# Moving the first copies, roots and transposes at two entries of the transformer blocks

## The chip, the cores and the metric

The kernel runs on one core of a Trainium2 chip. The metric is the device time of one execution in microseconds (us), as the median over several executions. The engines are TensorE (PE in the profile; PEld is its weight load), VectorE (DVE), ScalarE (ACT), GpSimd (POOL) and SyncE (SP), which issues most DMAs.

## The reference, cut to what matters

Two networks are run one behind the other on 512 rows of 1024 floats, all in float32. The first is a convolution layer and a retention layer with residuals, closed by an RMS normalisation. The second is two transformer blocks (`l` = 0, 1) over these rows and, in block 0, over 256 context rows too; each block has attention with local mixers and then a mixture of experts. The places that matter here are the two entries of a block, where rows are normalised, scaled and shifted, and multiplied by `w_in`:

```
return rms_norm(x, final_norm)                 # end of the first network
...
hx = x * (1 + sc1) + sh1                       # entry of block l
hc = ctx * (1 + mod_c[1]) + mod_c[0]
qx, kx, vx, ... = split(hx @ w_in[l])
kc, vc = split(hc @ w_in[l][:, ATTN_WIDTH:...])     # l = 1: context only feeds keys and values
...
y = hier_moe(tokens, ...)                      # end of block l
ctx = layer_norm(ALPHA * ctx + mod_c[5] * y[...], ln2_g[l], ln2_b[l])
x = layer_norm(ALPHA * x + g2 * y[...], ln2_g[l], ln2_b[l])
```

## The kernel before

Each engine has one program written out by hand; they meet only at semaphores, and each works through its program in order. Rows lie in tiles of 128: tiles 0 to 3 are x, tiles 4 and 5 are the context. Tile t is `xr[:, t, :]`, 128 rows by 1024.

Four entries into a half of a block are numbered `q` (0 and 2 are the entries of blocks 0 and 1 ahead of `w_in`; 1 and 3 those ahead of the mixture of experts). At each one every tile goes through the same steps. TensorE turns it in eight transposes of 128x128 (`mod_transposes(q, i_)`, line 1169) into two PSUM banks, 4 and 5 or 6 and 7 by turns for q = 0 and 2. `mod_copy(q, i_)` then scales, shifts and copies the eight blocks into `b_hxT`: for q = 0 ScalarE copies four (line 821) and VectorE four (line 1724); for q = 2 ScalarE copies all eight of tiles 0 to 4, and for the last tile both copy four. TensorE counts these copies (`hx_Ta`, `hx_Td`) before it uses a tile in a product with a chunk of `w_in` (line 1238). A product for a tile's queries is eight matmuls of 128x512 that add up in one bank; the trace has two records for each, so sixteen. Below, T(i) stands for the transposes of the i-th tile of an entry and P(i) for the i-th query product.

**Entry of block 0 (q = 0)**, called stage A below. The tiles are taken in the order 4, 5, 0, 1, 2, 3, since the context needs no statistics. VectorE adds the last product of the first network to the rows (`residual(1)`, line 1554), ScalarE sums squares (lines 722, 723), `rstd(2)` on VectorE (lines 1455, 1458) and `root(2)` on ScalarE (line 727) give the factor of each row, and VectorE multiplies four tiles (line 1654). There are six query products.

**Entry of block 1 (q = 2)**, stage B. `finish_rows` on VectorE has for each tile `stats_of(i_)`: three operations on 1024 columns that combine the two experts' results fetched by DMA into `c_y` (lines 2119 to 2121), two `bn_stats`, one `bn_aggr`, and one small addition (lines 1666 to 1669). ScalarE takes the root (`row_root`, line 828), and `norm(i_)` on VectorE (lines 1675, 1682) finishes the tile, after which its transposes may begin. There are only four query products here (tiles 0 to 3), but all six tiles are turned. Behind the query products come the products for keys and values (`kv`, six of 256 columns) and the rest of `w_in`. TensorE's own order is given by these lines:

```
for n, (c, kind, w, who) in enumerate(outs):
    while turned_tiles < min(n + 2, T):
        mod_transposes(2 * l, turned_tiles)
        turned_tiles += 1
```

Of the kernel before, what the change touches and what calls it, by code (L numbers as in the profile page):

```python
# [22 lines left out]
KD = D // P  # L23
# [90 lines left out]
def build(nc, a, out):  # L114
    ctx = ExitStack()
    with ctx:
# [4 lines left out]
        def sem(name):  # L121
            if name not in made:
                made[name] = ctx.enter_context(nc.semaphore(name))
            return made[name]
# [590 lines left out]
        def _(act):  # L715
# [94 lines left out]
                act.activation(stats[:, 24:28], stats[:, 16:20], ACT.Sqrt).then_inc(sem("ra_sd"), 1)  # L810

            sum_squares(2, mem(W0 + D, D), lambda t: act.wait_ge(sem("op_x"), past("op_x", 1) + 2 * (t + 1)))
            root(2)

            def mod_copy(q, i_):

                t = mod_order(q)[i_]
                g, b = hx_cols(q, int(t >= TX))
                act.wait_ge(sem("hx_t"), past("hx_t", q) + i_ + 1)
                for k in range(blocks_by_act(q, i_)):  # L820
                    m = act.activation(b_hxT[:, k, t * P:(t + 1) * P], bank(mod_bank(q, i_) + k // 4, P, (k % 4) * P),
                                       ACT.Identity, scale=g[:, k:k + 1], bias=b[:, k:k + 1])
                m.then_inc(sem("hx_Ta"), 1)

            def row_root(q, i_):

# [4 lines left out]
            for l in range(LAYERS):  # L831
# [1 line left out]
                nt = len(tiles)  # L833

                if l == 0:
                    for i_ in range(T):
                        mod_copy(0, i_)

                def queries_copied(i_):
# [123 lines left out]
                    outputs_copied(s, last[s], 1)  # L963

                for i_ in range(nt):
                    if l == 0 and i_ >= 2:
                        mod_copy(2, i_ - 2)
                    row_root(2 * l + 1, i_)
                if l == 0:
                    for i_ in range(nt - 2, nt):  # L970
                        mod_copy(2, i_)


        @block.tensor
        def _(pe):
# [196 lines left out]
            for l in range(LAYERS):  # L1172
# [37 lines left out]

                turned_tiles = 0
                for n, (c, kind, w, who) in enumerate(outs):
                    while turned_tiles < min(n + 2, T):
                        mod_transposes(2 * l, turned_tiles)
                        turned_tiles += 1
                    if n <= T:
                        copied = n + 1 if kind == "q" else T - 1 if n < 6 else T
                        pe.wait_ge(sem("hx_Ta"), past("hx_Ta", 2 * l) + copied)
                        pe.wait_ge(sem("hx_Td"), past("hx_Td", 2 * l) + copied)
                    if n == 0 or outs[n - 1][0] != c:  # L1220
                        g = base + c
                        pe.wait_ge(sem(f"st_w{g % 3}"), streamed(g))
                        wc = slot_cols(g)
                    b, m = out_bank(outs, n), last_in(outs, n)
                    if m is not None:
                        whom = outs[m][3]
                        pe.wait_ge(sem(f"in_{whom}"), past(f"in_{whom}", l) + taken(outs, m, whom))
                    for k in range(KD):
                        if kind in ("q", "g"):
                            o, l_, r_ = bank(b), b_hxT[:, k, w * P:(w + 1) * P], wc[:, k, :]  # L1230
                        elif kind == "kv":
                            o, l_, r_ = bank(b, 256), b_hxT[:, k, w * P:(w + 1) * P], wc[:, k, 0:256]
                        else:
                            f, part = w
                            t0, tn, _ = RANGE[part]
                            col = {"cb": 256, "cc": 0, "cx": 256}[kind] + f * P
                            o, l_, r_ = bank(b, tn), wc[:, k, col:col + P], b_hxT[:, k, t0:t0 + tn]
                        m = pe.matmul(o, l_, r_, start=(k == 0), stop=(k == KD - 1))  # L1238
                    m.then_inc(sem("in_mm"), 1)
                    if kind == "g":  # L1240
                        i_ = tiles.index(w)
                        if i_ == 0:
                            pe.wait_ge(sem("in_dve"), past("in_dve", l) + taken(outs, len(outs), "dve"))
                            pe.wait_ge(sem("ws"), past("ws", l) + 16)
                        turn_queries(i_)
                        turn_keys(i_)
                        if i_ >= 1:
                            mix(i_ - 1)
                        for t in more_keys(l, i_):
                            turn_keys(t, i_)  # L1250
                        if i_ >= 2:
                            turn_mixed(i_ - 2)
# [196 lines left out]
        def _(dve):  # L1449
# [197 lines left out]
                r_gate(h - 1)  # L1647
                r_norm(h)
            r_gate(RH - 1)
            residual(1)  # L1650
            rstd(2)
            dve.wait_ge(sem("op_x"), past("op_x", 1) + 8)
            for t in range(TX):
                dve.tensor_scalar(xr[:, t, :], xr[:, t, :], stats[:, 12 + t:13 + t], None, ALU.mult)\
                    .then_inc(sem("row_norm"), 1)

            def finish_rows(q, tiles, first, mod_q, free=None):

                nt = len(tiles)

                def stats_of(i_):
                    first(i_, tiles[i_])
                    for hf in range(2):
                        link(dve.bn_stats(stats[:, 100 + 12 * i_ + 6 * hf:106 + 12 * i_ + 6 * hf],
                                          xr[:, tiles[i_], hf * CW:(hf + 1) * CW]))
                    link(dve.bn_aggr(stats[:, 172 + 2 * i_:174 + 2 * i_], stats[:, 100 + 12 * i_:112 + 12 * i_]))
                    dve.tensor_scalar(stats[:, 184 + i_:185 + i_], stats[:, 173 + 2 * i_:174 + 2 * i_], LN_EPS, None,
                                      ALU.add).then_inc(sem("row_ve"), 1)  # L1670

                def norm(i_):
                    x_t = xr[:, tiles[i_], :]
                    dve.wait_ge(sem("row_sd"), past_rows(q) + i_ + 1)
                    link(dve.reciprocal(stats[:, 196 + i_:197 + i_], stats[:, 190 + i_:191 + i_]))
                    if mod_q is None:
                        link(dve.scalar_tensor_tensor(out=x_t, in0=x_t, scalar=stats[:, 172 + 2 * i_:173 + 2 * i_],
                                                      in1=b_ln[0], op0=ALU.subtract, op1=ALU.mult))
                        dve.scalar_tensor_tensor(out=x_t, in0=x_t, scalar=stats[:, 196 + i_:197 + i_], in1=b_ln[1],
                                                 op0=ALU.mult, op1=ALU.add).then_inc(sem("fin_x"), 1)  # L1680
                        return
                    dve.tensor_scalar(x_t, x_t, stats[:, 172 + 2 * i_:173 + 2 * i_], stats[:, 196 + i_:197 + i_],
                                      ALU.subtract, ALU.mult).then_inc(sem("row_norm"), 1)

                def rows(i_):
                    t = tiles[i_]
                    if free and t >= TX:
                        free()
                    dve.wait_ge(sem("row_norm"), past_norm(mod_q) + i_ + 1)
                    dve.tensor_tensor(b_hx[:, t, :], xr[:, t, :], b_mod[4 if t >= TX else 1], ALU.mult)\  # L1690
                        .then_inc(sem("hx_scaled"), 1)

                if mod_q == 2:
                    dve.sem_inc(sem("hx_Td"), T - 1)
                dve.wait_ge(sem("row_w"), 32 * (q + 1))
                dve.wait_ge(sem("fin_x"), past_full(q) + (TX if q % 2 == 0 else nt))
                for i_ in range(nt):
                    stats_of(i_)
                    if free:
                        if i_ >= 1:  # L1700
                            mod_copy(mod_q, i_ - 1)
                        norm(i_)
                        if 1 <= i_ < nt - 1:
                            rows(i_ - 1)
                        continue
                    if i_ >= 1:
                        norm(i_ - 1)
                if mod_q is None:
                    norm(nt - 1)
                elif mod_q == 2:  # L1710
                    norm(nt - 1)
                    mod_copy(mod_q, nt - 1)
                else:
                    mod_copy(mod_q, nt - 1)
                    for i_ in range(nt - 2, nt):
                        rows(i_)

            def mod_copy(q, i_):
# [7 lines left out]
                                            g[:, k:k + 1], b[:, k:k + 1], ALU.mult, ALU.add)  # L1726
                ins.then_inc(sem("hx_Td"), 1)

            dve.wait_ge(sem("rows_in"), 80)
            for i_ in range(T):  # L1730
                mod_copy(0, i_)
            for l in range(LAYERS):
                tiles, outs = full(l), in_outputs(l)
# [569 lines left out]
```

## Time and profile before

| what | value |
| --- | --- |
| median of 3 runs | 3088.6 us (3087.21 to 3092.43) |
| the profiled execution | 3091.9 us, its span 3090.1 us |
| mean granted TensorE clock | 0.942 of full speed |
| TensorE busy | 2755.0 us, 89% of the span |
| VectorE, ScalarE, GpSimd busy | 1063.4, 460.4, 317.6 us |
| chain that ended last | TensorE 71%, SyncE's queue 12%, DMA 7%, VectorE 5% |

Times in the rows are microseconds from the start of the span. A row of the timeline has the start, the length, the engine, the line, the operation, what it writes and reads, the number of merged instructions, and in brackets the idle time of the engine ahead of it and what ended it. Merged rows of one line can span short pauses between their instructions.

### The profile page before, as it was taken

Reading aid. Unit: us, or ns where it says so; the run is one execution under the profiler, and the core shown is the slowest. Engines: PE = TensorE matmul, PEld = TensorE weight load, DVE = VectorE, ACT = ScalarE, POOL = GpSimd, SP = SyncE. Lnnn points to the kernel's source line nnn. Section 1 sums busy time; section 2 is a strip of 40 time slices with the busy share of each in tenths; the row PEclk is TensorE's granted clock in tenths of the full one; section 3 lists DMA queues with packets and bytes.
Section 4 is the critical chain, followed back from the end, with each engine's and each line's share of the span. In section 5 each row is a group of like instructions: output and inputs, shape, how many; then the busy total and the mean of one; then the engine's idle time right before and its main releaser. Section 6 shows DMA issues by size and latency. Waiting matters only on the chain.

```text
span 3090.1 us, 33083 instructions
## 1 busy us (share of the span) xinstructions
PE 2755.0 (89%) x11436; PEld 1254.1 (41%) x11436; DVE 1063.4 (34%) x2065; ACT 460.4 (15%) x874; POOL 317.6 (10%) x445
## 2 busy tenths in 40 slices
PE   7999999999998999999699977886999688999773
PEld 3444444444444456564433322233555333333221
DVE  5998960330012042455531111115454521111104
ACT  3111130100111010551101100002151000111000
POOL 0101021000000000001122211110000121222110
PEclk9999999999999999899799998997989699999886
DMA  6665341222120311001699999974201799779993
GB/s 232 206 204 178 108 178 56 99 82 82 60 76 1 120 55 46 10 1 70 242 356 363 387 393 392 392 269 181 99 1 50 276 390 371 259 274 365 394 359 131
DMA packets 272218, 603.12 MB, mean 195 GB/s; under 512 B 18437, under 2 KB 43333, under 8 KB 272001
## 3 DMA queue, kind: packets, MB, share of 16 engines
q1 hardware_dynamic: 256864, 580.70, 51.5%
q0 software_dynamic: 15264, 21.24, 2.0%
q8 instruction: 56, 0.92, 0.1%
q14 instruction: 34, 0.27, 0.0%
HBM read 743.04 MB, written 29.20 MB: 250 GB/s over the span
## 4 chain that ended last, share of the span: by engine, by line
PE 71%; SPq 12%; DMA 7%; DVE 5%; issue 2%; ACT 2%; POOL 0%; POOLq 0%; DVEq 0%; ACTq 0%
PE psum L1404 11%; PE psum L1019 11%; PE psum L1106 11%; SPq L657 10%; PE psum L1238 9%; PE psum L1077 7%; DMA arena<-in_w 6%; PE psum L1342 4%; PE psum L1426 4%; PE psum L1285 2%; PE psum L1274 2%; PE psum L1004 1%; PE psum L1127 1%; PE psum L1297 1%; PE psum L1391 1%
## 5 line engine op out<-in xcount | busy, mean ns | idle before, releaser
L1404 PE MATMUL psum<-arena 128*64 128x512 f32 x2656 | 651.2, 636 | 120.2 <-DMA arena<-in_w 118.5
L1404 PEld LDWEIGHTS psum<-arena 128*64 128x64 f32 x2656 | 197.0, 145 | 454.0 <-issue 448.8
L1019 PE MATMUL psum<-arena 128*128 128x512 f32 x768 | 341.2, 600 | 2.6 <-ACTq L754 2.6
L1106 PE MATMUL psum<-arena 128*128 128x512 f32 x768 | 329.9, 592 | 0.8 <-ACT arena L733 0.8
L1426 PE MATMUL psum<-arena 128*64 128x512 f32 x1328 | 301.8, 598 | 0.2 <-issue 0.2
L1503 DVE SCALAR_TENSOR_TENSOR arena<-arena 128x512 f32<-128x512 f32 x451 | 300.2, 749 | 0.0
L1238 PE MATMUL psum<-arena 128*128 128x512 f32 (+1 forms) x800 | 289.6, 522 | 4.2 <-issue 4.2
L1077 PE MATMUL psum<-arena 128*128 128x512 f32 x512 | 224.6, 602 | 5.2 <-POOL arena L2173 4.4
L1106 PEld LDWEIGHTS psum<-arena 128*128 128x128 f32 x768 | 145.8, 190 | 184.2 <-issue 183.2
L1019 PEld LDWEIGHTS psum<-arena 128*128 128x128 f32 x768 | 143.4, 191 | 177.1 <-issue 174.3
L1238 PEld LDWEIGHTS psum<-arena 128*128 128x128 f32 x800 | 152.3, 192 | 128.8 <-issue 121.1
L2082 DVE COPY arena<-psum 128x256 f32<-128x256 f32 x83 | 35.2, 425 | 418.9 <-PE psum L1415 418.7
L2092 DVE SCALAR_TENSOR_TENSOR arena<-arena,psum 64x512 f32<-64x512 f32 x83 | 61.4, 740 | 330.4 <-ACT arena L957 330.4
L1426 PEld LDWEIGHTS psum<-arena 128*64 128x64 f32 x1328 | 96.3, 138 | 191.2 <-issue 191.1
L957 ACT ACTIVATE arena<-psum 64x512 f32<-64x512 f32 x83 | 49.4, 595 | 806.5 <-PE psum L1404 806.5
L1077 PEld LDWEIGHTS psum<-arena 128*128 128x128 f32 x512 | 98.7, 193 | 130.1 <-issue 128.9
L1342 PE MATMUL psum<-arena 128*128 128x512 f32 x320 | 139.2, 594 | 3.4 <-ACT arena L906 3.4
L2075 DVE COPY arena<-psum 128x512 f32<-128x512 f32 x89 | 61.5, 691 | 208.2 <-PE psum L1391 208.2
L2214 POOL DMA_INDIRECT arena<-moe_in,arena x95 | 101.1, 1064 | 83.0 <-POOL arena L2211 80.4
L2211 POOL COPY arena<-arena 128x1 int32 (+1 forms) x95 | 17.8, 188 | 805.2 <-PE psum L1391 759.3
L1285 PE MATMUL psum<-arena 128*128 128x128 f32 x640 | 87.3, 289 | 9.4 <-issue 4.8
L2230 POOL DMA_INDIRECT moe_out<-arena x83 | 85.0, 1024 | 94.9 <-issue 53.9
(279 smaller groups left out, 2051.6 us busy)
## 6 DMA issues: line engine op xcount, KB each, us to landing
arena<-in_w SPq DMA_DIRECT2D x261, 2048.0 KB
arena<-in_w_ada SPq DMA_DIRECT2D x48, 1024.0 KB, 5.2
arena<-in_conv_w_in SPq DMA_DIRECT2D x24, 1024.0 KB
arena<-in_ret_w_in SPq DMA_DIRECT2D x12, 2048.0 KB, 8.0
arena<-in_w_in SPq DMA_DIRECT2D x8, 2048.0 KB, 9.0
arena<-moe_out SPq DMA_DIRECT2D x10, 1024.0 KB, 9.7
arena<-in_conv_w_out SPq DMA_DIRECT2D x4, 2048.0 KB, 11.9
arena<-in_ret_w_out SPq DMA_DIRECT2D x4, 2048.0 KB, 7.8
```

Of the source, the lines that this page charges most:

```text
L657: sp.dma_start(m_w[s][j], ws[j][:, bass.ds(e * kk[j], kk[j]), :], cond=new)\
L1019: m = pe.matmul(bank(b + c), w[:, k, c * P:(c + 1) * P], c_hT[:, k, :], start=(k == 0), stop=(k == KD - 1))
L1077: m = pe.matmul(bank(2 * t + hf), mem(y + S * k + P * t, P), slot_rows(n)[:, k % 4, hf * CW:(hf + 1) * CW], start=(k == 0), stop=(k == KI ...
L1106: m = pe.matmul(bank(4 * (n % 2) + j), l_, r_, start=(k == 0), stop=(k == KD - 1))
L1238: m = pe.matmul(o, l_, r_, start=(k == 0), stop=(k == KD - 1))
L1285: m = pe.matmul(bank(4 + kv, P, hh * P), b_sb[i % 2][:, 4 * kv + hh, c * P:(c + 1) * P], b_dg[i % 2][:, 4 * kv + hh, :], start=True, stop= ...
L1342: m = pe.matmul(bank(2 * (t % 2) + hf), y[:, t * P:(t + 1) * P], slot_rows(base + 4 + k // 4)[:, k % 4, hf * CW:(hf + 1) * CW], start=(k = ...
L1404: m = pe.matmul(bank(2 * s)[part], m_xsT[s][:, at:at + SB], m_w[s][j][:, k, :], start=(k == 0), stop=(k == KD - 1))
L1426: m = pe.matmul(bank(2 * s + 1)[SB * hf:SB * hf + SB], m_hT[s][:, k, :], m_w[s][2][:, k, hf * CW:(hf + 1) * CW], start=(k == 0), stop=(k = ...
L1503: ins = dve.scalar_tensor_tensor(out=acc, in0=u, scalar=w[:, j:j + 1], in1=acc, op0=ALU.mult, op1=ALU.add)
L2214: pool.indirect_dma_start(out=m_xs[s], in_=halves_in, out_offset=None, in_offset=bass.IndirectOffsetOnAxis(m_gi[s], 0), bounds_check=2 * n ...
L2230: pool.indirect_dma_start(out=halves_out, in_=m_y[s], in_offset=None, out_offset=bass.IndirectOffsetOnAxis(m_si[s], 0), bounds_check=4 * n ...
```

## The change

Three things are moved; nothing is computed that was not computed before, and no operation is added or removed.

1. Stage A: VectorE and ScalarE copy the first turned tile (`mod_copy(0, 0)`, tile 4) ahead of `rstd(2)` and `root(2)`, not behind them.
2. Stage B: VectorE normalises tiles 0, 1 and 2 directly behind their own statistics, and no longer one tile later; tiles 3 to 5 as before. On ScalarE the copy of tile 0 now stands ahead of the root of tile 1, the copy of tile 1 ahead of the root of tile 2, and from tile 3 on the root stands ahead of the copy.
3. Stage B: TensorE's T(n+1) stands in the middle of P(n), behind four of its eight matmuls, and not ahead of P(n). Stage A keeps its order there.

```
--- before.py
+++ after.py
@@ -810,7 +810,6 @@
                 act.activation(stats[:, 24:28], stats[:, 16:20], ACT.Sqrt).then_inc(sem("ra_sd"), 1)
 
             sum_squares(2, mem(W0 + D, D), lambda t: act.wait_ge(sem("op_x"), past("op_x", 1) + 2 * (t + 1)))
-            root(2)
 
             def mod_copy(q, i_):
 
@@ -822,6 +821,9 @@
                                        ACT.Identity, scale=g[:, k:k + 1], bias=b[:, k:k + 1])
                 m.then_inc(sem("hx_Ta"), 1)
 
+            mod_copy(0, 0)
+            root(2)
+
             def row_root(q, i_):
 
                 act.wait_ge(sem("row_ve"), past_rows(q) + i_ + 1)
@@ -833,7 +835,7 @@
                 nt = len(tiles)
 
                 if l == 0:
-                    for i_ in range(T):
+                    for i_ in range(1, T):
                         mod_copy(0, i_)
 
                 def queries_copied(i_):
@@ -963,12 +965,13 @@
                     outputs_copied(s, last[s], 1)
 
                 for i_ in range(nt):
-                    if l == 0 and i_ >= 2:
-                        mod_copy(2, i_ - 2)
+                    if l == 0 and 1 <= i_ < 3:
+                        mod_copy(2, i_ - 1)
                     row_root(2 * l + 1, i_)
+                    if l == 0 and i_ >= 3:
+                        mod_copy(2, i_ - 1)
                 if l == 0:
-                    for i_ in range(nt - 2, nt):
-                        mod_copy(2, i_)
+                    mod_copy(2, nt - 1)
 
 
         @block.tensor
@@ -1210,7 +1213,7 @@
 
                 turned_tiles = 0
                 for n, (c, kind, w, who) in enumerate(outs):
-                    while turned_tiles < min(n + 2, T):
+                    while turned_tiles < min(n + 2 if l == 0 or kind != "q" else n + 1, T):
                         mod_transposes(2 * l, turned_tiles)
                         turned_tiles += 1
                     if n <= T:
@@ -1235,6 +1238,9 @@
                             t0, tn, _ = RANGE[part]
                             col = {"cb": 256, "cc": 0, "cx": 256}[kind] + f * P
                             o, l_, r_ = bank(b, tn), wc[:, k, col:col + P], b_hxT[:, k, t0:t0 + tn]
+                        if k == KD // 2 and l == 1 and kind == "q":
+                            mod_transposes(2 * l, turned_tiles)
+                            turned_tiles += 1
                         m = pe.matmul(o, l_, r_, start=(k == 0), stop=(k == KD - 1))
                     m.then_inc(sem("in_mm"), 1)
                     if kind == "g":
@@ -1647,13 +1653,6 @@
                 r_gate(h - 1)
                 r_norm(h)
             r_gate(RH - 1)
-            residual(1)
-            rstd(2)
-            dve.wait_ge(sem("op_x"), past("op_x", 1) + 8)
-            for t in range(TX):
-                dve.tensor_scalar(xr[:, t, :], xr[:, t, :], stats[:, 12 + t:13 + t], None, ALU.mult)\
-                    .then_inc(sem("row_norm"), 1)
-
             def finish_rows(q, tiles, first, mod_q, free=None):
 
 
@@ -1703,7 +1702,9 @@
                         if 1 <= i_ < nt - 1:
                             rows(i_ - 1)
                         continue
-                    if i_ >= 1:
+                    if mod_q == 2 and i_ < 3:
+                        norm(i_)
+                    elif i_ >= (4 if mod_q == 2 else 1):
                         norm(i_ - 1)
                 if mod_q is None:
                     norm(nt - 1)
@@ -1726,8 +1727,16 @@
                                             g[:, k:k + 1], b[:, k:k + 1], ALU.mult, ALU.add)
                 ins.then_inc(sem("hx_Td"), 1)
 
+            residual(1)
+            mod_copy(0, 0)
+            rstd(2)
+            dve.wait_ge(sem("op_x"), past("op_x", 1) + 8)
+            for t in range(TX):
+                dve.tensor_scalar(xr[:, t, :], xr[:, t, :], stats[:, 12 + t:13 + t], None, ALU.mult)\
+                    .then_inc(sem("row_norm"), 1)
+
             dve.wait_ge(sem("rows_in"), 80)
-            for i_ in range(T):
+            for i_ in range(1, T):
                 mod_copy(0, i_)
             for l in range(LAYERS):
                 tiles, outs = full(l), in_outputs(l)
```

Stage A on ScalarE; L722 and L723 are the sums of squares, L727 is the root, L821 (L820 after the change) the copies of turned tiles, L870 and L872 later copies. Before:

```order
L722 ACTIVATE arena<-arena 128x1024 x4
L723 ACTIVATE arena<-arena 128x1
L727 ACTIVATE arena<-arena 128x4
L821 ACTIVATE arena<-psum,arena 128x128 x24
L870 ACTIVATE arena<-psum 128x512
```

and with the change:

```order
L722 ACTIVATE arena<-arena 128x1024 x4
L723 ACTIVATE arena<-arena 128x1
L820 ACTIVATE arena<-psum,arena 128x128 x4
L727 ACTIVATE arena<-arena 128x4
L820 ACTIVATE arena<-psum,arena 128x128 x20
L872 ACTIVATE arena<-psum 128x512
```

Four of the 24 copies, those of tile 4, have moved ahead of the root. VectorE's program changes in the same way around L1455 and L1458.

Stage B on ScalarE; L828 (L830 after the change) is the root of one tile, preceded by a load of its function table, L821 (L820) the copies. Before:

```order
L828 ACT_TABLE_LOAD
L828 ACTIVATE arena<-arena 128x1 x2
L821 ACTIVATE arena<-psum,arena 128x128 x8
L828 ACTIVATE arena<-arena 128x1
L821 ACTIVATE arena<-psum,arena 128x128 x8
L828 ACTIVATE arena<-arena 128x1
L821 ACTIVATE arena<-psum,arena 128x128 x8
L828 ACTIVATE arena<-arena 128x1
L821 ACTIVATE arena<-psum,arena 128x128 x8
L828 ACTIVATE arena<-arena 128x1
L821 ACTIVATE arena<-psum,arena 128x128 x12
```

and with the change:

```order
L830 ACT_TABLE_LOAD
L830 ACTIVATE arena<-arena 128x1
L820 ACTIVATE arena<-psum,arena 128x128 x8
L830 ACTIVATE arena<-arena 128x1
L820 ACTIVATE arena<-psum,arena 128x128 x8
L830 ACTIVATE arena<-arena 128x1 x2
L820 ACTIVATE arena<-psum,arena 128x128 x8
L830 ACTIVATE arena<-arena 128x1
L820 ACTIVATE arena<-psum,arena 128x128 x8
L830 ACTIVATE arena<-arena 128x1
L820 ACTIVATE arena<-psum,arena 128x128 x12
```

The pair of roots without a copy between them has moved from tiles 0 and 1 to tiles 2 and 3.

Stage B on TensorE; L1169 (L1172) are transposes, L1238 (L1244) the products, of 512 columns for queries and 256 for keys and values. Before:

```order
L1169 MATMUL psum<-arena 128x128 x16
L1238 MATMUL psum<-arena 128x512 x8
L1169 MATMUL psum<-arena 128x128 x8
L1238 MATMUL psum<-arena 128x512 x8
L1169 MATMUL psum<-arena 128x128 x8
L1238 MATMUL psum<-arena 128x512 x8
L1169 MATMUL psum<-arena 128x128 x8
L1238 MATMUL psum<-arena 128x512 x8
L1169 MATMUL psum<-arena 128x128 x8
L1238 MATMUL psum<-arena 128x256 x48
```

and with the change:

```order
L1172 MATMUL psum<-arena 128x128 x8
L1244 MATMUL psum<-arena 128x512 x4
L1172 MATMUL psum<-arena 128x128 x8
L1244 MATMUL psum<-arena 128x512 x8
L1172 MATMUL psum<-arena 128x128 x8
L1244 MATMUL psum<-arena 128x512 x8
L1172 MATMUL psum<-arena 128x128 x8
L1244 MATMUL psum<-arena 128x512 x8
L1172 MATMUL psum<-arena 128x128 x8
L1244 MATMUL psum<-arena 128x512 x4
L1172 MATMUL psum<-arena 128x128 x8
L1244 MATMUL psum<-arena 128x256 x48
```

T(0) now stands alone, each of T(1) to T(4) stands between the halves of P(0) to P(3), and T(5) stands ahead of the key and value products as before.

## Rows read from the trace of the kernel before

**Rows 1.** The page: the span, and the chain that ended last by engine.
```profile
span 3090.1 us, 33083 instructions
...
PE 71%; SPq 12%; DMA 7%; DVE 5%; issue 2%; ACT 2%; POOL 0%; POOLq 0%; DVEq 0%; ACTq 0%
```

**Rows 2.** Timeline of TensorE at the entry of block 0 (stage A).
```profile
1094.34 1.94 PE L1169 MATMUL psum<-arena 128*128 128x128 f32 x16 [0.83 <-issue]
1100.53 9.60 PE L1238 MATMUL psum<-arena 128*128 128x512 f32 x16 [4.25 <-issue]
...
1110.84 7.03 PE L1238 MATMUL psum<-arena 128*128 128x512 f32 x16
```

**Rows 3.** Timelines of VectorE and of ScalarE in stage A.
```profile
1096.41 2.74 DVE L1654 TENSOR_SCALAR arena<-arena 128x1024 f32<-128x1024 f32 x4
1099.06 2.64 DVE L1724 TENSOR_SCALAR arena<-psum,arena 128x128 f32<-128x128 f32 x8
1111.04 1.37 DVE L1724 TENSOR_SCALAR arena<-psum,arena 128x128 f32<-128x128 f32 x4 [9.34 <-PE psum L1169]
...
1095.52 0.20 ACT L723 ACTIVATE arena<-arena 128x1 f32<-128x1 f32 x1
...
1111.04 1.51 ACT L821 ACTIVATE arena<-psum,arena 128x128 f32<-128x128 f32 x4 [12.08 <-PE psum L1169]
```

**Rows 4.** Stretches: length, busy by engine (count), granted TensorE clock, DMA share, GB/s.
```profile
1096.30:1100.50 4.20, 0.00 (x0) 0.00 (x1) 4.17 (x10) 2.66 (x8) 0.00 (x0) 0.79 1.04 400
1100.50:1105.60 5.10, 5.07 (x6) 2.17 (x7) 1.20 (x4) 0.00 (x0) 0.00 (x0) 0.50 0.03 12
...
2071.90:2074.20 2.30, 0.01 (x1) 0.00 (x1) 0.69 (x1) 0.16 (x1) 1.26 (x3) 1.00 0.00 0
...
2075.70:2080.00 4.30, 4.26 (x14) 1.48 (x16) 0.76 (x2) 0.00 (x0) 0.74 (x1) 0.69 0.89 282
```

**Rows 5.** Timeline of TensorE at the entry of block 1 (stage B).
```profile
2113.88 1.97 PE L1169 MATMUL psum<-arena 128*128 128x128 f32 x8 [26.35 <-DVE arena L1682]
...
2122.11 9.04 PE L1238 MATMUL psum<-arena 128*128 128x512 f32 x16
2130.98 1.04 PE L1169 MATMUL psum<-arena 128*128 128x128 f32 x8
2131.86 7.03 PE L1238 MATMUL psum<-arena 128*128 128x512 f32 x16
...
2155.08 1.25 PE L1238 MATMUL psum<-arena 128*128 128x256 f32 x5
```

**Rows 6.** Timeline of VectorE in stage B.
```profile
2101.74 1.22 DVE L2119 TENSOR_TENSOR arena<-arena 128x1024 f32<-128x1024 f32 x1 [25.22 <-DMA arena<-moe_out]
...
2107.29 1.21 DVE L2119 TENSOR_TENSOR arena<-arena 128x1024 f32<-128x1024 f32 x1
...
2113.01 0.81 DVE L1682 TENSOR_SCALAR arena<-arena 128x1024 f32<-128x1024 f32 x1
...
2143.03 0.81 DVE L1682 TENSOR_SCALAR arena<-arena 128x1024 f32<-128x1024 f32 x1
```

**Rows 7.** Timeline of ScalarE in stage B.
```profile
2088.27 1.28 ACT L828 ACT_TABLE_LOAD   x1
2107.41 0.20 ACT L828 ACTIVATE arena<-arena 128x1 f32<-128x1 f32 x1 [17.85 <-DVE arena L1669]
...
2115.89 2.90 ACT L821 ACTIVATE arena<-psum,arena 128x128 f32<-128x128 f32 x8 [2.74 <-PE psum L1169]
...
2142.56 0.23 ACT L828 ACTIVATE arena<-arena 128x1 f32<-128x1 f32 x1
```

**Rows 8.** The first chunk of block 1's `w_in`, and TensorE's wait behind stage B.
```profile
L575 SPq DMA_DIRECT2D arena<-in_w_in x1: 379/379/379, 2089.0 to 2089.0; - x1
...
DMA to landing us min/median/max: 9.9/9.9/9.9
...
2168.91 7.20 PEld L1238 LDWEIGHTS psum<-arena 128*128 128x128 f32 x34 [0.25 <-DVE arena L1760]
```

More of the change, by code:

```diff
@@ L812, in _ @@
             sum_squares(2, mem(W0 + D, D), lambda t: act.wait_ge(sem("op_x"), past("op_x", 1) + 2 * (t + 1)))
-            root(2)
             def mod_copy(q, i_):
@@ L823, in mod_copy @@
                 m.then_inc(sem("hx_Ta"), 1)
+            mod_copy(0, 0)
+            root(2)
             def row_root(q, i_):
@@ L835, in _ @@
                 if l == 0:
-                    for i_ in range(T):
+                    for i_ in range(1, T):
                         mod_copy(0, i_)
@@ L965, in _ @@
                 for i_ in range(nt):
-                    if l == 0 and i_ >= 2:
-                        mod_copy(2, i_ - 2)
+                    if l == 0 and 1 <= i_ < 3:
+                        mod_copy(2, i_ - 1)
                     row_root(2 * l + 1, i_)
+                    if l == 0 and i_ >= 3:
+                        mod_copy(2, i_ - 1)
                 if l == 0:
-                    for i_ in range(nt - 2, nt):
-                        mod_copy(2, i_)
+                    mod_copy(2, nt - 1)
         @block.tensor
@@ L1212, in _ @@
                 for n, (c, kind, w, who) in enumerate(outs):
-                    while turned_tiles < min(n + 2, T):
+                    while turned_tiles < min(n + 2 if l == 0 or kind != "q" else n + 1, T):
                         mod_transposes(2 * l, turned_tiles)
@@ L1237, in _ @@
                             o, l_, r_ = bank(b, tn), wc[:, k, col:col + P], b_hxT[:, k, t0:t0 + tn]
+                        if k == KD // 2 and l == 1 and kind == "q":
+                            mod_transposes(2 * l, turned_tiles)
+                            turned_tiles += 1
                         m = pe.matmul(o, l_, r_, start=(k == 0), stop=(k == KD - 1))
@@ L1649, in _ @@
             r_gate(RH - 1)
[L1650 to L1655, printed above, removed]
             def finish_rows(q, tiles, first, mod_q, free=None):
@@ L1705, in finish_rows @@
                         continue
-                    if i_ >= 1:
+                    if mod_q == 2 and i_ < 3:
+                        norm(i_)
+                    elif i_ >= (4 if mod_q == 2 else 1):
                         norm(i_ - 1)
@@ L1727, in mod_copy @@
                 ins.then_inc(sem("hx_Td"), 1)
+            residual(1)
+            mod_copy(0, 0)
+            rstd(2)
+            dve.wait_ge(sem("op_x"), past("op_x", 1) + 8)
+            for t in range(TX):
+                dve.tensor_scalar(xr[:, t, :], xr[:, t, :], stats[:, 12 + t:13 + t], None, ALU.mult)\
+                    .then_inc(sem("row_norm"), 1)
             dve.wait_ge(sem("rows_in"), 80)
-            for i_ in range(T):
+            for i_ in range(1, T):
                 mod_copy(0, i_)
```

## The prediction

> **What bounds the kernel now.** I read the page first: TensorE carries 71% of the chain that ended last in a span of 3090.1 us [rows 1], so a microsecond that TensorE stands idle or slow in a stage is a microsecond of the end, unless a later wait takes it back. Then the timelines of the two stages, engine by engine, to see what TensorE waits for there, and last the granted clock.
>
> Stage A. T(0) and T(1) are turned in 1.94 us from 1094.34, so until 1096.28; P(0) starts at 1100.53 after 4.25 idle [rows 2]. On VectorE the four normalisations (1096.41, 2.74 long) stand ahead of the copies, and the eight copies of the first two tiles run 2.64 from 1099.06 [rows 3]. Four copies take 1.37 [rows 3], so tile 4's are done at 1100.43, and P(0) starts 0.10 later. That is the last-ending wait. In the idle stretch the granted clock falls (mean 0.79), and it is 0.50, or 1.2 GHz, for the next 5.1 us [rows 4]; P(0) takes 9.60 against 7.03 for P(1) [rows 2], so the fall costs 2.57.
>
> Stage B. VectorE starts when the experts' results arrive at 2101.74 and comes to the second tile at 2107.29, a step of 5.55 per tile without its normalisation [rows 6]. T(0) waits for the normalisation of tile 0, which stands behind the statistics of tile 1 and ends at 2113.01 + 0.81 = 2113.82; T(0) starts at 2113.88 [rows 5, 6]. P(0) starts at 2122.11, behind T(1), and from there TensorE has no pause up to the first key product at 2155.08 [rows 5]. So VectorE sets the start and TensorE itself the rest: tile 5 is normalised by 2143.84 [rows 6], eleven microseconds before the key products. The steady step of a query product with one set of transposes is (2155.08 - 2131.86)/3 = 7.74, of which the transposes take 2131.86 - 2130.98 = 0.88 and the product 6.86 [rows 5]. The first transposes take 1.97 at half rate against 1.04 [rows 5].
>
> **Stage A, part by part.** T(0) alone takes 1.04 [rows 5], so it is done at about 1095.38. VectorE, free after the residual, copies its half in 1.37, to 1096.75. ScalarE's last sum of squares and its small copy end at 1095.52 + 0.20 = 1095.72; its half takes 1.51 [rows 3], to 1097.23. P(0) then starts at about 1097.33 instead of 1100.53: 3.20 earlier. The gap falls from 4.25 to 1.05. What I take: with so short a gap the clock stays full, and the 2.57 come back too. Sum of stage A: 5.8; if the clock falls all the same, 3.2.
>
> What is delayed: the statistics of tiles 0 to 3 wait for tile 4's copies. The root goes from before 1096.2 to about 1097.3, the four normalisations to about 1097.7 to 1100.4, and the second tile's copies on VectorE to 1101.8. TensorE wants the first normalised tile at the end of P(0), 1097.33 + 6.86 = 1104.2, and the second tile's copies one T later: cover of 6 and 3 us. Cost nothing; without that cover it would be the 1.4 of the copies moved ahead.
>
> **Stage B, part by part.** VectorE is free after tile 0's statistics at about the same moment as before, and the root of tile 0 starts at 2107.41 [rows 7]. From the start of a root to the end of the normalisation takes 2143.84 - 2142.56 = 1.28 [rows 6, 7]: tile 0 is done at 2108.69 and T(0) starts at 2108.75. ScalarE's copy began 2.01 behind the start of T(0) and took 2.90 [rows 5, 7], so it ends at 2113.66, and P(0) may start at 2113.75, **8.36 earlier**, since T(1) no longer stands ahead of it. Its weights landed at 2089.0 + 9.9 = 2098.9 [rows 8].
>
> From there I follow the chain that ends last, which is no longer TensorE's own. P(0) starts at half rate. The cost of a start was 2.57 in stage A, and 9.75 - 7.74 + 0.93 = 2.94 in stage B with the slow T(1) counted [rows 5]; I take 2.6, all of it in the first half of P(0). That half takes 3.43 + 2.6 and ends at 2119.8, T(1) at 2120.8 (tile 1 is normalised at about 2115.4, so it does not wait). ScalarE copies tile 1 to 2123.75. Only then comes the root of tile 2, whose statistics were ready at about 2120.9: VectorE idles 2.9. Tile 2 is done at 2125.0, tile 3's statistics at 2130.5, its root at 2130.8, and only then does ScalarE copy tile 2, to 2133.7, though T(2) was done at about 2128.5. This is the new stall: P(1) runs 2124.1 to 2131.85 and P(2) starts at 2133.8, after 1.9 idle. From P(2) on VectorE keeps up (tile 3 normalised at 2137.1 for a T(3) wanted at 2137.2, which is tight; tile 4 at 2143.5 for 2145.1), so the key products start at 2133.8 + 2 x 7.74 + 0.88 = 2150.15 against 2155.08: **4.9 earlier**. Of the 8.36, about 0.9 go back to T(1), which now lies behind the start of P(0), 1.9 to the stall, and the rest to the slow clock, which now meets more of the work.
>
> Behind the stage two things could take it back. TensorE waits 0.25 for VectorE's rotation of the first queries at 2168.9 [rows 8]; VectorE reaches it from T(5) through the last tile's copies, so it moves with T(5). The later chunks of weights are asked for as TensorE frees their place, and move too.
>
> Bounds of stage B: if P(0)'s first half and T(1) run wholly at half rate, T(1) ends 1.8 later and 3.1 are left; if the clock falls in the new pause as well, another start of 2.6 is paid and 0.5 is left. If the clock is high from the start, tile 2's root waits for its statistics alone (2120.9), P(2) starts at 2131.0, and 7.7 are gained.
>
> **A rule weighed.** ScalarE's program alternates a root and copies in stage B. In the rows the table is loaded once, 1.28 us at 2088.27, and later roots follow copies with 0.2 us of their own work and no load between [rows 7]. The Trainium skill, "ScalarE: Activation LUTs", section "What ACT_TABLE_LOAD costs", says that every switch to a function of a different set costs a load of about 1.28 us and a drain of about as much again; with the three switches that my chain holds (copy of tile 0, root of tile 2, copy of tile 2) that would be an estimated 8 us, more than stage B gives. The rows decide: root and copy share what is loaded, and the order shows one load there as before. The sum takes nothing for it.
>
> **Sum.** 5.8 + 4.9 = 10.7. Against the profiled execution that is 3091.9 - 10.7 = 3081.2. That execution stands 3.3 above the median, so for a median I predict 3088.6 - 10.7 = **3077.9 us**, 0.35% faster.
>
> **The rivals.**
> *The clock falls in stage A all the same.* In the pause of 2.3 us at 2071.9 TensorE was idle at full clock, and in the stretch from 2075.7 the clock was 0.69 [rows 4]: a pause does not need to be 4 us long. Against it: stage A's pause is half of that. Then the gain is 3.2 + 4.9 = 8.1: 3080.5.
> *Stage B brings little.* The new pause of 1.9 is close to that one of 2.3. If the clock falls in it, or P(0) is slow throughout, stage B brings 0.5 to 3.1, in all 6.3 to 8.9: 3079.7 to 3082.3.
> *A later wait takes stage B back*, so that it gives nothing at the end: TensorE's wait for the rotation would have to grow by what was gained. Then 5.8 are left: 3082.8, within 0.2%. If stage A's clock is lost too, 3085.4. For it speaks only that 0.25 are waited there already.
> *TensorE stays slow in stage B: slower than before.* With P(0) started early and every half product followed by a chance to wait, its work is thinner, and the clock may stay at 1.2 GHz. Each product then costs 6.86 more and each T about 0.93. It decides against the change once the slow stretch holds 10.7/6.86, about 1.6, more products than in my sum. All four products and five T slow cost 4 x 6.86 + 5 x 0.93 - 2.6 = 29.5 more, less 2 for pauses that the slow products swallow: about 3105. Against it: in both stages the clock rose during P(0) [rows 2, 4, 5], and P(0) to P(1) have no pause.
>
> **How the numbers follow.** Chances: the forecast 0.62, with a range of its own from 3075 to 3081; the clock lost in stage A 0.13; stage B short 0.10; a later wait 0.10; slower 0.05. About 0.2%, 6.2 us, is what can be told from no change. The first three are faster by more, save a little of the third; I put 0.83 on faster, 0.12 on the same, 0.05 on slower. The bounds of the terms give gains of 3.7 to 13.5, so 3075.1 to 3084.9; runs of the kernel before lie from 3087.21 to 3092.43, so I widen below and reach to 3072.5, and above to 3084.5, which leaves out the slow case and the edge of the fourth.
>
> **What would show it.** In the new profile's stage A: VectorE and ScalarE copy four blocks each ahead of the root; TensorE's pause ahead of P(0) is about 1 us, P(0) takes about 7.0, and T(2) does not wait. In stage B: T(0) starts about 7.0 behind the first combine; P(0)'s first half about 5 behind T(0); a pause of about 2 ahead of P(2) that ends with ScalarE's copy, and a pause of about 3 on VectorE ahead of tile 2's reciprocal; the first key product about 48.4 behind the first combine, where it was 53.3. The prediction fails if P(0) in either stage is slow for longer than before, if VectorE or a weight chunk holds TensorE behind the stage, or if another stage changes in length.

## The result and the profile after

The kernel with the change takes 3074.84 us in the median of 6 runs (3071.71 to 3081.5), the kernel before 3092.14 in 6 runs beside it (3087.21 to 3092.64). The ratio is 0.995, with a 95% interval from 0.994 to 0.996: 12 to 19 us faster where 10.7 was forecast. Two later comparisons of the same kernel gave 0.996 [0.9947, 0.9974] and 0.9959 [0.9946, 0.9973], about 12.5 us; their intervals, about 8 to 17 us, hold the 10.7.

The timeline of TensorE at the entry of block 0, with the change, answers to [rows 2]:

```profile
1095.28 1.94 PE L1172 MATMUL psum<-arena 128*128 128x128 f32 x16 [0.83 <-issue]
1098.10 7.13 PE L1244 MATMUL psum<-arena 128*128 128x512 f32 x16 [0.88 <-ACT arena L820]
1105.07 1.04 PE L1172 MATMUL psum<-arena 128*128 128x128 f32 x8
1105.94 7.03 PE L1244 MATMUL psum<-arena 128*128 128x512 f32 x16
```

P(0) starts 2.82 behind T(0) where it was 6.19, after a pause of 0.88 that ends with ScalarE's copy, and takes 7.13 instead of 9.60. The start of P(1) is 10.66 behind T(0) where it was 16.50: **5.84 gained**. The VectorE and ScalarE timelines of the same place answer to [rows 3]:

```profile
1096.39 1.36 DVE L1725 TENSOR_SCALAR arena<-psum,arena 128x128 f32<-128x128 f32 x4 [1.21 <-PE psum L1172]
1098.39 2.74 DVE L1735 TENSOR_SCALAR arena<-arena 128x1024 f32<-128x1024 f32 x4
1101.04 1.36 DVE L1725 TENSOR_SCALAR arena<-psum,arena 128x128 f32<-128x128 f32 x4
...
1096.56 1.49 ACT L820 ACTIVATE arena<-psum,arena 128x128 f32<-128x128 f32 x4
1097.93 0.21 ACT L727 ACTIVATE arena<-arena 128x4 f32<-128x4 f32 x1
```

Both halves of tile 4 are copied ahead of the root. The normalisations start at 1098.39 and the second tile's copies end at 1102.4, while TensorE wants them at 1105.94: the delay is covered.

In stage B the timeline of TensorE answers to [rows 5]:

```profile
2104.30 1.97 PE L1172 MATMUL psum<-arena 128*128 128x128 f32 x8 [22.85 <-DVE arena L1681]
2109.26 5.69 PE L1244 MATMUL psum<-arena 128*128 128x512 f32 x8 [2.99 <-ACT arena L820]
2114.78 1.04 PE L1172 MATMUL psum<-arena 128*128 128x128 f32 x8
2115.66 7.03 PE L1244 MATMUL psum<-arena 128*128 128x512 f32 x16
...
2123.40 3.60 PE L1244 MATMUL psum<-arena 128*128 128x512 f32 x8
2128.51 3.70 PE L1244 MATMUL psum<-arena 128*128 128x512 f32 x8 [1.51 <-ACT arena L820]
2132.04 1.04 PE L1172 MATMUL psum<-arena 128*128 128x128 f32 x8
2132.91 7.03 PE L1244 MATMUL psum<-arena 128*128 128x512 f32 x16
...
2144.97 7.29 PE L1244 MATMUL psum<-arena 128*128 128x256 f32 x33
```

The product at 2109.26 is the first half of P(0), partly at half rate; those at 2123.40 and 2128.51 are the second half of P(1) and the first of P(2), and between them lies the new pause, 1.51, which ends with ScalarE's copy. A row of 7.03 holds the second half of one product and the first half of the next. VectorE's timeline there, to be held against [rows 6], gives the origin and the cause of that pause:

```profile
2097.33 1.23 DVE L2128 TENSOR_TENSOR arena<-arena 128x1024 f32<-128x1024 f32 x1 [26.98 <-DMA arena<-moe_out]
...
2103.43 0.81 DVE L1681 TENSOR_SCALAR arena<-arena 128x1024 f32<-128x1024 f32 x1
...
2118.88 0.16 DVE L1674 RECIPROCAL arena<-arena 128x1 f32<-128x1 f32 x1 [2.28 <-ACT arena L830]
2119.08 0.81 DVE L1681 TENSOR_SCALAR arena<-arena 128x1024 f32<-128x1024 f32 x1
...
2131.07 0.81 DVE L1681 TENSOR_SCALAR arena<-arena 128x1024 f32<-128x1024 f32 x1
```

and ScalarE's, to be held against [rows 7]:

```profile
2115.86 2.90 ACT L820 ACTIVATE arena<-psum,arena 128x128 f32<-128x128 f32 x8 [5.84 <-PE psum L1172]
2118.61 0.24 ACT L830 ACTIVATE arena<-arena 128x1 f32<-128x1 f32 x1
2125.46 0.20 ACT L830 ACTIVATE arena<-arena 128x1 f32<-128x1 f32 x1 [6.62 <-DVE arena L1668]
2125.57 2.88 ACT L820 ACTIVATE arena<-psum,arena 128x128 f32<-128x128 f32 x8
```

Tile 2's root (2118.61) waits behind tile 1's copy (2115.86), so VectorE stands for 2.28; that makes tile 3's statistics late, tile 3's root comes at 2125.46, and tile 2's copy stands behind it. From the first combine (2097.33) to the first key product (2144.97) are 47.64 against 53.34 [rows 5, 6]: **5.70 gained**.

The two stages give 11.5. The two profiled spans, 3090.1 and 3074.4, differ by 15.7. So some 4 us of this pair of traces lie where nothing was edited, and the experiments had to say what they are. One pair of traces is not enough for that: a second trace of the kernel before, taken later, has a span of 3086.0, only 11.6 longer than that of the change.

### The profile page after: what moved, and what is told of

Read it like the earlier page. It is cut to its first block, busy times and chain, and to the rows that moved or that the text cites. A ratio compares the mean times of both kernels' runs of the same rounds, so it can differ in the third digit from the quotient of the medians.

```text
span 3074.4 us, 33083 instructions
## 1 busy us (share of the span) xinstructions
PE 2743.3 (89%) x11436; PEld 1248.1 (41%) x11436; DVE 1062.8 (35%) x2065; ACT 459.4 (15%) x874; POOL 316.7 (10%) x445
## 4 chain that ended last, share of the span: by engine, by line
PE 71%; SPq 12%; DMA 8%; DVE 5%; issue 2%; ACT 2%; POOL 0%; POOLq 0%; DVEq 0%; ACTq 0%
PE psum L1022 11%; PE psum L1410 11%; PE psum L1109 11%; SPq L657 10%; PE psum L1244 9%; PE psum L1080 7%; DMA arena<-in_w 6%; PE psum L1348 4%; PE psum L1432 4%; PE psum L1291 3%; PE psum L1280 2%; PE psum L1007 1%; PE psum L1130 1%; PE psum L1303 1%; PE psum L1397 1%
## 5 line engine op out<-in xcount | busy, mean ns | idle before, releaser
L1244 PE MATMUL psum<-arena 128*128 128x512 f32 (+1 forms) x800 | 287.7, 519 | 5.4 <-ACT arena L820 5.4
L1244 PEld LDWEIGHTS psum<-arena 128*128 128x128 f32 x800 | 151.1, 191 | 128.6 <-issue 113.1
```

## The experiments

In all of them ratios are against runs of the kernel before on the same chip. "Entry B" is the time from the first combine to the first key product of block 1. In the four traces in which stage B is as before (the two of the kernel before, stage A alone, the filled pause) it is 52.8 to 53.4, so differences of half a microsecond between single traces say nothing.

**The halves by themselves, and both kernels again.** The first kernel has only the edits of stage A:

```
-            root(2)                      # ScalarE
+            mod_copy(0, 0)
+            root(2)
...
             residual(1)                  # VectorE
+            mod_copy(0, 0)
             rstd(2)
```

> Only the edits of stage A. Theory L (only the two stages change, the rest of the difference is chance): P(0) of block 0 starts 3.2 us earlier and takes about 7.1 instead of 9.6, so the kernel gains 5.8 us, about 0.19%. Rival S (gains at an entry grow later, because later stages follow in another way): more than 8 us. Rival C (the clock falls in the pause in most executions and the traced one was lucky): 3.2 us.

Measured: 0.9981 [0.997, 0.9993], which of 3088.85 us is 5.9 gained, from 2.2 to 9.3. TensorE's timeline of it:

```profile
1096.62 1.94 PE L1171 MATMUL psum<-arena 128*128 128x128 f32 x16 [0.83 <-issue]
1099.45 7.13 PE L1240 MATMUL psum<-arena 128*128 128x512 f32 x16 [0.89 <-ACT arena L820]
```

The pause and the length of P(0) are those of the whole change, so in this execution the rival in which the clock falls did not occur. The time alone could not exclude it: the interval holds its 3.2, and gains of 8 to 9 by rival S too. The second kernel has only the edits of stage B (the lines of `finish_rows`, of ScalarE's last loop and of TensorE's two places in the diff above):

> Only the edits of stage B. Theory L: from the first combine to the first key product 47.6 us as with the whole change, where before it was 53.3, so 5.7 us gained, about 0.18%. Rival S: 9 to 11 us, since 5 of the microseconds that the whole change gained beyond my sum lay behind stage B. Half of the stage given back later: 3 us.

Measured: 0.9986 [0.9974, 0.9998], 4.3 us. Its entry B is 2152.41 - 2104.07 = 48.34, so 5.0 shorter than 53.34. Its interval is 0.6 to 8.0 us: the 9 to 11 of rival S are excluded, the rival with 3 is not. Theory L fits both kernels. Two rows of its TensorE timeline give the first half of P(0):

```profile
2116.00 6.38 PE L1242 MATMUL psum<-arena 128*128 128x512 f32 x8 [2.99 <-ACT arena L821]
2122.21 1.04 PE L1170 MATMUL psum<-arena 128*128 128x128 f32 x8
```

Up to T(1) that half takes 6.21 here and 5.52 in the whole change, and the two entries differ by the same 0.7 (48.34 and 47.64).

> The whole change once more. Theory L: 11.5 us on average, and in another trace the gain outside the two stages is another one than the 4 to 5 us of the first trace, of either sign. Rival S: 15 to 17 us, and the same stages (behind 1280, 2257 to 2270, 2870) are shorter again by the same amounts.

Measured: 0.996 [0.9947, 0.9974], 12.4 us; entry B is 2144.92 - 2097.00 = 47.92. The time lies nearer to L's 11.5, but its interval, 8.0 to 16.4, holds much of S's 15 to 17 too. The trace speaks for S: L expected another difference outside the two stages, and it was the same as in the first trace (the table below).

> The kernel before, unchanged, beside itself. Theory L: a ratio of 1.000, and its trace differs from the first one by 1 to 5 us in the stretches where the clock falls and in the mixtures of experts. Rival S: its trace agrees with the first within 1 us in these stretches.

Measured: 1.0007 [0.9996, 1.0018]; entry B 2153.49 - 2100.42 = 53.07. Its trace agrees with that of before within 0.1 us in the three stretches of the table below, as S expected, and differs by 2.7 in the last one (from about 2804 to 3042, 238.3 and 235.6), as L expected. It also comes to stage A 1.8 us earlier. So single traces of one kernel do differ by some microseconds, but in other places than those where the change gained.

**Stage B in its two parts.** First TensorE's new order alone:

```
-                    while turned_tiles < min(n + 2, T):
+                    while turned_tiles < min(n + 2 if l == 0 or kind != "q" else n + 1, T):
...
+                        if k == KD // 2 and l == 1 and kind == "q":
+                            mod_transposes(2 * l, turned_tiles)
+                            turned_tiles += 1
```

> Of stage B only TensorE's new order, VectorE and ScalarE as before. My working applied to this order: P(0) starts 1 us after ScalarE's copy of tile 0, at 17.2 us behind the first combine instead of 20.4, and the first key product at 51.6 instead of 53.3: a gain of 1.7 us. Rival (the order on TensorE alone makes the gain of stage B): 4 us or more. Rival (splitting a product costs something by itself): no gain or a loss.

Measured: entry B 2153.82 - 2102.93 = 50.89, so 2.4 shorter than before (1.7 expected), P(0) 17.1 behind the first combine; the ratio is 0.9998 [0.9987, 1.0009], which cannot tell 2.4 us (0.9992) from nothing. Then the rows alone:

```
+                    if mod_q == 2 and i_ < 3:                   # VectorE
+                        norm(i_)
+                    elif i_ >= (4 if mod_q == 2 else 1):
                         norm(i_ - 1)
...
-                    if l == 0 and i_ >= 2:                      # ScalarE
-                        mod_copy(2, i_ - 2)
+                    if l == 0 and 1 <= i_ < 3:
+                        mod_copy(2, i_ - 1)
                     row_root(2 * l + 1, i_)
+                    if l == 0 and i_ >= 3:
+                        mod_copy(2, i_ - 1)
...
```

> Of stage B only the earlier normalisations and the order of roots and copies, TensorE as before. My working: T(0) 7.0 behind the first combine, T(1) 13.6, P(0) 15.5 and the first key product 49 behind it instead of 53.3: a gain of 4 to 4.5 us, no pause ahead of P(2). Rival (both parts are needed): under 2 us.

Measured: entry B 2152.56 - 2103.53 = 49.03, 4.3 shorter, with 0.9989 [0.9977, 1.0002]. The interval holds no gain at all too, so that each part gains rests on its trace, not on its time. In the traces the two parts give 2.4 and 4.3 and together 5.0 to 5.7: less than their sum, since the pause of 1.5 ahead of P(2) appears only with both.

**The clock term of stage A by itself.** The kernel before, with the pause filled:

```
+                    if l == 0 and n == 0:
+                        for k in range(38):
+                            pe.transpose(bank(0, P, (k % 4) * P), xr[:, 4, ...], ident)
```

> The kernel before with 38 more transposes of tile 4 into an unused bank, about 4.1 us of TensorE's work, in the pause ahead of P(0) of stage A; the output does not change. If the clock term of 2.57 is right, P(0) starts where it did and takes 7.0 to 7.1 instead of 9.6: 2.5 us gained. Rival (the first product after such a pause is slow for another reason, its weights or its first reading): it stays near 9.6 and nothing is gained.

Measured: 0.9982 [0.997, 0.9995], 5.6 us; the interval, 1.5 to 9.3 us, holds the 2.5 forecast. Its timeline of TensorE:

```profile
1096.33 4.31 PE L1218 MATMUL psum<-arena 128*128 128x128 f32 x38
1100.74 7.11 PE L1241 MATMUL psum<-arena 128*128 128x512 f32 x16
```

Nothing is earlier here: P(0) waits for the same copies as in [rows 2], and only the idle time ahead of it is gone. It takes 7.11 instead of 9.60, with a granted clock of 1.00 where [rows 4] have 0.50. The rival, that weights or the first reading make it slow, falls, since neither was touched. So the slowness was that of the clock, and the 2.5 are shown. The trace is another 2.6 shorter in the attention of block 0 (about 1272 to 1302 before), where nothing was edited.

**A better order of roots.** From the trace after I took the one pause that was left:

```
-                    if mod_q == 2 and i_ < 3:                   # VectorE
+                    if mod_q == 2 and i_ < 4:
                         norm(i_)
-                    elif i_ >= (4 if mod_q == 2 else 1):
+                    elif i_ >= (5 if mod_q == 2 else 1):
...
-                    if l == 0 and 1 <= i_ < 3:                  # ScalarE
+                    if l == 0 and i_ == 1:
                         mod_copy(2, i_ - 1)
                     row_root(2 * l + 1, i_)
-                    if l == 0 and i_ >= 3:
+                    if l == 0 and i_ >= 2:
                         mod_copy(2, i_ - 1)
```

> The whole change, and on ScalarE the root of tile 2 ahead of the copy of tile 1, and tile 3 normalised directly behind its statistics as well. By the trace with the change ScalarE's root then waits for no copy, VectorE loses its 2.3 us pause, TensorE waits about 0.6 for the copy of tile 1 ahead of P(1) and nothing ahead of P(2): the first key product 46.5 behind the first combine instead of 47.6, 1.1 us gained over the change. Rival (the pause only moves to another product): 47.6 or later.

> The version with the root put first once more. The key products again start 46.8 behind the first combine against 47.6; if the stretches behind fall as in its first trace (31.2 in attention of block 1), no gain over the change: 0.996 of the kernel before. If they vary from run to run, anything between 0.994 and 0.997.

Measured: entry B is 2142.25 - 2095.47 = 46.78 and 2140.33 - 2093.78 = 46.55, about 1.1 to 1.3 shorter than with the change (47.64, 47.92, and 47.88 in the third trace). Ahead of P(2) there is no pause. In the first trace P(0) ran slow for longer (its first half 6.44 up to T(1)) and hid ScalarE's copy; in the second (4.95) there is a pause of 1.00 ahead of P(1). The ratios are 0.9955 [0.994, 0.997] and 0.996 [0.9947, 0.9974]: no difference from the change that these runs can tell. The stretches behind did vary here between two traces of one kernel: in attention of block 1 the first has 31.1, the second 27.9, and in the experts behind it 158.7 and 155.7.

**Does the place of the work against the clock matter?** 16 transposes ahead of the first key product of block 1, in each kernel:

```
+                    if l == 1 and n == 4:
+                        for k in range(16):
+                            pe.transpose(bank(4, P), xr[:, 4, (k % 8) * P:(k % 8 + 1) * P], ident)
```

> The kernel before with 16 more transposes, 1.7 us of TensorE's work, ahead of the first key product of block 1; the output does not change. Theory M (the work behind moves against the moments at which the clock changes, and with it how long attention of block 1 runs at half rate): the stretch from 88 us behind the first key product, 31.2 us long before, changes by 1 to 4 us, and the granted clock in it too; the kernel is not simply 1.7 slower. Theory N (that stretch has one length, and what the change gained there came through another wait): it stays 31.2 and all is 1.7 later.

> The kernel with the change and the same 16 transposes at the same place. Theory M: the stretch of attention of block 1, 27.9 to 28.1 us in both traces with the change, goes back towards 31 us, as with the root put first, where the work behind came 2.7 us earlier; about 4 us slower than with the change alone. Theory N: it stays at 28 and the kernel is 1.7 us slower than with the change alone.

> The whole change a third time. If what lies outside the two stages is fixed by the program, its trace has the stretch of attention of block 1 at 28 us again and the one of the mixture of experts behind it 2.8 shorter than before; if it is chance, one of them differs. The ratio 0.995 to 0.996.

Measured: 0.9996 [0.9981, 1.0011] for the kernel before with them, 0.9974 [0.9965, 0.9984] with the change and them, 0.9959 [0.9946, 0.9973] for the change a third time. So the change with the transposes was about 4.6 us slower than the change alone, near the 4 of theory M, but the two intervals overlap and do not exclude N's 1.7; for the kernel before the interval of the ratio holds both theories. The stretches, each from the same matmul to the same matmul by their count from the start of the program, are these (us; the granted clock in brackets):

| kernel | attention of block 0 | attention of block 1 | experts of block 1, first 160 us |
| --- | --- | --- | --- |
| before | 30.1 (0.72) | 31.2 (0.73) | 158.7 (0.91) |
| before again | 30.1 (0.72) | 31.1 (0.73) | 158.7 (0.91) |
| before, 16 transposes | 30.1 (0.72) | 32.1 (0.68) | 159.0 (0.91) |
| before, pause filled | 27.5 (0.81) | 30.9 (0.72) | 158.5 (0.91) |
| stage A alone | 29.1 (0.77) | 27.7 (0.88) | 159.0 (0.91) |
| stage B alone | 30.1 (0.72) | 32.1 (0.68) | 155.8 (0.95) |
| of B only TensorE's order | 30.1 (0.72) | 31.8 (0.69) | 156.3 (0.91) |
| of B only the rows | 30.1 (0.72) | 31.1 (0.73) | 158.6 (0.91) |
| the change | 29.0 (0.76) | 27.9 (0.88) | 155.9 (0.95) |
| the change again | 29.1 (0.77) | 28.1 (0.88) | 155.9 (0.95) |
| the change, third | 26.3 (0.94) | 28.0 (0.88) | 155.8 (0.93) |
| the change, 16 transposes | 26.9 (0.87) | 27.0 (0.94) | 158.3 (0.91) |
| root first | 29.0 (0.76) | 31.1 (0.73) | 158.7 (0.91) |
| root first again | 29.1 (0.77) | 27.9 (0.88) | 155.7 (0.95) |

Three of the rows behind it, of before, of the change, and of the change with 16 transposes (length, busy time by engine, granted clock, DMA share, GB/s):

```profile
2242.40:2273.60 31.20, 25.57 (x102) 16.40 (x102) 13.69 (x52) 14.73 (x31) 0.00 (x0) 0.73 0.00 1
```

```profile
2232.30:2260.20 27.90, 22.03 (x102) 14.28 (x101) 13.90 (x51) 14.59 (x30) 0.00 (x0) 0.88 0.00 1
```

```profile
2231.20:2258.20 27.00, 21.13 (x102) 13.79 (x102) 13.56 (x52) 14.60 (x31) 0.00 (x0) 0.94 0.00 1
```

The same 102 matmul records keep TensorE busy for 25.57, 22.03 or 21.13, while VectorE and ScalarE do the same work in nearly the same time. So theory N falls: in attention the length follows the granted clock in both columns, to within 0.2 us. In the experts' column it does so less well: 156.3 at 0.91 with TensorE's order alone, 155.8 at 0.93 and 0.95. Theory M's mechanism is seen in attention, but both its forecasts for that stretch failed: the 16 transposes made the attention of block 1 only 0.9 longer in the kernel before, and with the change it became shorter, not longer; the 2.4 that came back lie in the experts' stretch. The change alone then held one more surprise: the attention of block 0 had 29.0, 29.1 and 26.3 in its three traces.

## Why the prediction was right

**Stage A** came out as worked: 5.8 forecast, 5.84 in the trace, 5.9 [2.2, 9.3] by time. The 3.20 were 3.37 and the clock term 2.57 was 2.47, since P(0) took 7.13; the filled pause shows that term by itself (7.11). The pause of 1.05 was 0.88, and the rival in which the clock falls all the same did not occur in any of the traces with these edits. The cover of the delayed normalisations held.

**Stage B** was forecast step by step at 48.4 from the first combine to the first key product; traced are 47.64, 47.92 and 47.88, and 48.34 in stage B alone. T(0) was to start 7.0 behind the combine and did so after 6.97; P(0) 12.0 and 11.93. Two terms were off. P(0)'s first half was set to 6.03 up to T(1); it took 5.52, 5.79 and 5.75 in the three traces of the change and 6.21 in stage B alone, and entry B less that half is 42.1 in all four. So the entry varies with how long P(0) runs slow. The other term is the stall ahead of P(2), 1.9 against 1.51 to 1.53 in all four, however long that half took: on ScalarE a root or copy begins 0.1 us before the row ahead of it ends (2118.61 against 2115.86 + 2.90), which the sum did not have. The cause of the stall was as forecast, the root of tile 2 behind the copy of tile 1, with a VectorE pause of 2.28 for 2.9. T(3) was called tight and was: tile 3 is normalised at 2131.07 + 0.81 = 2131.88, and T(3) starts at 2132.04 without a wait. The clock did not fall in the pause ahead of P(2), in which the granted clock is 1.00,

```profile
2127.00:2128.40 1.40, 0.00 (x0) 0.00 (x0) 1.37 (x2) 1.40 (x5) 0.00 (x0) 1.00 0.00 0
```

and behind it T(3) takes 1.04 and the second half of P(2) with the first of P(3) 7.03. TensorE's wait for VectorE's rotation stayed at 0.2, so the later wait did not come, and the slow stage of the fourth rival did not either: the clock rose during P(0) as before.

**The rule on table loads** (the Trainium skill, "ScalarE: Activation LUTs", section "What ACT_TABLE_LOAD costs") is for a switch to a function of a different set, and was rightly kept out of the sum: this trace has copies directly ahead of the root at 2118.61 and directly behind the one at 2125.46, and no load between.

**What the sum lacked** are the 1.7 to 4.8 us that came on top, by the ratios of the three comparisons (12.4, 12.7 and 15.5 us against 10.7); only the first interval excludes 10.7. The sum took everything behind and between the two entries as a shift. In the traces with the change, set against the first trace of the kernel before, attention of block 1 is 3.1 to 3.3 shorter, the experts behind it 2.8 to 2.9 and attention of block 0 1.0 to 3.8; the rest of the experts is 1.0 longer, and VectorE waited 26.98 instead of 25.22 for the results ahead of stage B. The two in attention go with the granted clock, the one in the experts only roughly; the last two also differ between the two traces of the kernel before (the last stretch by 2.7, the wait 25.22 and 26.25), so they cannot be put down to the change. None of them holds an edit. I had named the clock only within the two stages; "another stage changes in length" stood among the signs that the prediction fails, without a size, and that sign did appear. So the two stages came out by their mechanism, and the assumption that all else only shifts was wrong, by 1.0 to 3.8 us in each of three stretches.

That the total still lies 3.1 from the forecast is partly luck: 3077.9 was counted from 3088.6, the median of three runs, and the six runs beside the change had 3092.14. From there 10.7 less would be 3081.4, and 3074.84 is 6.6 below that.

What decides in which of these stretches the clock falls is not settled. The two traces of the kernel before agree in all three stretches and those of the change in two, which speaks against mere chance; but the two traces with the root first differ in two, and delaying the work on purpose did not move the stretches as the theory had it.

## What to carry to other kernels

Follow the chain through every engine that a reordered step queues behind: here the walk from TensorE's transposes over ScalarE's copy and root to VectorE and back gave the new pause and its place before anything was run. A pause of several microseconds ahead of a long run of matmuls can cost twice, once as itself and once in the slow start behind it. And where the clock falls several times in a program, stretches that a change does not touch can differ by 3 us between two traces, so compare stage by stage, in more than one trace of each kernel, before you explain a total.

## What the runs showed of the hardware that was not expected

Filling a pause of 4.25 us with 38 transposes whose result nobody reads made the kernel 0.18% faster [0.05%, 0.3%], about as much as the reordering of stage A; in its trace stage A is 2.5 us shorter and the attention of block 0 is 2.6 shorter. The granted clock mostly behaved alike in repeats: in both traces of the kernel before, the attention stretches had 0.72 and 0.73, and in all three with the change the one of block 1 had 0.88. With the root first it had 0.73 once and 0.88 once, and in block 0 the change had 0.76, 0.77 and 0.94. And a pause of 1.51 at full clock in stage B, or 0.88 in stage A, was not followed by a slow product, while the one of 4.25 was.
